# Hybrid decoder layer: expert outputs gated and split into three bf16 parts for a one-hot combination, second-layer bias added once after the expert loop, gates turned ahead of layer two

## The reference, cut to what matters

```python
def expert_block(args):
    xe, e = args
    hid = xe @ w1[e] + b1[e]
    gate = jnp.minimum(hid[:, :D_EXPERT], SWIGLU_LIMIT)
    up = jnp.clip(hid[:, D_EXPERT:], -SWIGLU_LIMIT, SWIGLU_LIMIT)
    act = gate * jax.nn.sigmoid(SWIGLU_ALPHA * gate) * (up + 1.0)
    return act @ w2[e] + b2[e]
yb = lax.map(expert_block, (xb, block_e)).reshape(rows, d) * row_gate[:, None]
return jnp.zeros((n + 1, d), h.dtype).at[row_tok].add(yb)[:n]
```

## Time and profile before

| what | value |
|---|---|
| median of three runs | 1681.19 us (1679.02 to 1683.44) |
| the profiled execution, its own time | 1679.4 us |
| the profiled execution, its span | 1677.6 us |
| PE busy | 1612.6 us (96%) |
| DVE, ACT, POOL busy | 458.6, 316.9, 112.1 us |
| mean granted clock of TensorE | 0.987 |
| chain that ended last | PE 72%, DMA 21%, DVE 4% |
| DMA | 477.32 MB, mean 285 GB/s |

### The profile page before, as it was taken

The page is one execution under the profiler, slowest core; times in us unless marked ns, Lnnn a source line. Parts: engine busy times, 40 slices in busy tenths (PEclk is TensorE's granted clock), DMA queues, the critical chain, the costliest instruction groups (busy, mean ns, idle before and its releaser), DMA issues.

```text
span 1677.6 us, 21022 instructions
## 1 busy us (share of the span) xinstructions
PE 1612.6 (96%) x8487; PEld 751.6 (45%) x8488; DVE 458.6 (27%) x966; ACT 316.9 (19%) x529; POOL 112.1 (7%) x150
## 2 busy tenths in 40 slices
PE   7999999999979999999999999999999999999997
PEld 4677776776555433333333333333333333333332
DVE  3665322224771421111111112111121111112122
ACT  2224131123400131111111111111011111111123
POOL 1322101012150030000000000000000000000000
PEclk9999999999989999999999999999999999999999
DMA  4334212125854579996999999999999979949940
GB/s 160 111 121 128 102 51 102 51 101 163 255 150 168 240 285 420 417 378 258 419 419 416 419 417 418 419 416 419 417 418 419 416 311 364 419 194 408 415 146 31
DMA packets 112366, 477.32 MB, mean 285 GB/s; under 512 B 7386, under 2 KB 18067, under 8 KB 79475
## 3 DMA queue, kind: packets, MB, share of 16 engines
q1 hardware_dynamic: 109846, 467.64, 70.4%
q0 software_dynamic: 2480, 9.11, 1.9%
HBM read 469.72 MB, written 6.62 MB: 284 GB/s over the span
## 4 chain that ended last, share of the span: by engine, by line
PE 72%; DMA 21%; DVE 4%; issue 1%; ACT 1%; SPq 0%; ACTq 0%; DVEq 0%
PE ps L631 69%; DMA arena<-in_moe_w 20%; PE ps L981 1%; ACT arena L1307 1%; PE ps L1053 1%; DVE arena L1525 1%; PE ps L649 0%; DMA arena<-in_state_conv 0%; DVE arena L1620 0%; DVE arena L1559 0%; DVE arena L1522 0%; PE ps L1087 0%; PE ps L703 0%; DVE arena L1563 0%; DVE arena L1589 0%
## 5 line engine op out<-in xcount | busy, mean ns | idle before, releaser
L631 PE MATMUL ps<-arena 128*64 128x512 f32 (+12 forms) x7898 | 1521.4, 476 | 37.8 <-DMA arena<-in_moe_w 17.0
L631 PEld LDWEIGHTS ps<-arena 128*64 128x64 f32 (+6 forms) x7898 | 687.0, 148 | 842.0 <-issue 663.3
L1774 DVE TENSOR_SCALAR arena<-ps 128x512 f32<-128x512 f32 x35 | 24.2, 692 | 446.2 <-PE ps L631 446.2
L1322 ACT ACTIVATE arena<-arena 128x512 f32<-128x512 f32 x35 | 22.0, 630 | 475.4 <-DVE arena L1774 475.4
L1767 DVE COPY arena<-arena 96x64 bf16 x35 | 6.7, 191 | 251.6 <-PE ps L1053 248.1
L1327 ACT ACTIVATE arena<-ps 128x512 f32<-128x512 f32 x35 | 20.9, 597 | 261.6 <-PE ps L631 261.6
L1758 DVE TENSOR_TENSOR arena<-ps,arena 128x512 f32<-128x512 f32 x36 | 24.9, 692 | 122.7 <-PE ps L981 121.6
L1307 ACT ACTIVATE arena<-ps 128x512 f32<-128x512 f32 x36 | 21.5, 597 | 134.4 <-PE ps L631 134.4
L1322 ACT ACT_TABLE_LOAD x35 | 44.9, 1283 | 0.6
L1409 DVE SCALAR_TENSOR_TENSOR arena<-arena 128x344 f32<-128x344 f32 x48 | 35.5, 740 | 1.7
L1120 ACT ACTIVATE arena<-arena 128x1024 f32<-128x1024 f32 (+1 forms) x12 | 12.6, 1052 | 113.8 <-DVE arena L1644 103.3
(11 more groups left out here) (249 smaller groups left out, 649.3 us busy)
## 6 DMA issues: line engine op xcount, KB each, us to landing
arena<-in_moe_w SPq DMA_DIRECT2D x192, 2048.0 KB, 18.3
arena<-in_w_in SPq DMA_DIRECT2D x16, 2048.0 KB, 11.1
arena<-in_state_delta POOLq DMA_DIRECT2D x16, 512.0 KB, 6.3
arena<-in_w_proj_a SPq DMA_DIRECT2D x2, 2048.0 KB, 11.1
out_sd_s<-arena SPq DMA_DIRECT2D x8, 512.0 KB, 5.8
arena<-in_w_proj_b SPq DMA_DIRECT2D x2, 2048.0 KB, 11.5
arena<-in_w_out SPq DMA_DIRECT2D x2, 2048.0 KB, 7.8
arena<-in_ple_gate_w SPq DMA_DIRECT2D x2, 2048.0 KB, 16.0
```

What stands on the lines that cost most here:

```text
L631: return pe.matmul(out, lhsT, rhs, start=first, stop=last, skip_group_check=True)
L1322: ACTF(s_sb, g_sb, ACT.Sigmoid, scale=ALPHA).then_inc(sem("glu_sig_ready"), 1)
L1774: TS(g_sb, ps[:, GATE_B, :], LIMIT, None, ALU.min).then_inc(sem("glu_gate_ready"), 1)
```

## The change

On PE, in a block: `combine` now multiplies a bf16 one-hot `PgT` (1 where a slot takes a token) by three bf16 parts of y that have been multiplied by the slot's gate, so 18 bf16 matmuls in place of 6 f32 ones. The gates are turned directly behind the activation (`turn_gates`), where the rows were turned; the rows are turned between the two units of layer two. The layer-two bias leaves the loop: after it, `gmT` (expert by token, f32, 32 rows) times `b2` is added for all tokens in 6 f32 matmuls ahead of the last `combine`. `b2` is read by one more DMA (128 KB) in front of `ptok`, into the slot of u3, and the PE queue waits for all of `ple_in` before these matmuls, where it waited behind `combine`.

On DVE: a reduce of the turned gates over the tokens gives the slot's gate `gate_col`; `PgT` is "greater than zero" of the same bank; the remainders of the split are made by two more instructions. On ACT: y's copy out of PSUM becomes the scaled first part, and a second part is rounded from the remainder; the copy of `PgT` is gone. `UP_B` is free again for the next block when DVE has made the first remainder (`ysb_ready` at `b * 4 + 2`). At the start, DVE clears four buffers in place of one, and the biases' split on POOL has 2048 columns in place of 3072.

```diff
@@ SP
-            sp.dma_start(b12[0:NE, 2 * D:3 * D], t["moe_b2"][0]).then_inc(sem("router_in"), 16)
@@
             sp.wait_ge(used[uslot[3]], nb)
+            sp.dma_start(b2[0:NE, :], t["moe_b2"][0]).then_inc(sem("ple_in"), 16)
             sp.dma_start(ptok[:, 0:2, :], t["p_prompt"][0, 0].rearrange("(a p) d -> p a d", p=P)).then_inc(sem("ple_in"), 16)
@@ PE
-                pe.wait_ge(sem("ysb_ready"), ready)
-                pe.wait_ge(sem("pgT_ready"), ready)
+                pe.wait_ge(sem("ysb_ready"), ready * 4)
                 for tt in range(2):
+                    for part in y_parts:
+                        for g in range(2):
+                            mm(ps[:, 2 * tt + g, :], PgT[64 * g:64 * g + 64, P * tt:P * tt + P], part[64 * g:64 * g + 64, :], False, True)
+                for part in y_parts:
                     for g in range(2):
-                        mm(ps[:, 2 * tt + g, :], PgT[64 * g:64 * g + 64, P * tt:P * tt + P], y_sb[64 * g:64 * g + 64, :], False, True)
-                for g in range(2):
-                    m = mm(ps[64 * g:64 * g + 64, 4, :], PgT[64 * g:64 * g + 64, 2 * P:TOK], y_sb[64 * g:64 * g + 64, :], False, True)
+                        m = mm(ps[64 * g:64 * g + 64, 4, :], PgT[64 * g:64 * g + 64, 2 * P:TOK], part[64 * g:64 * g + 64, :], False, True)
                 m.then_inc(sem("comb_done"), 1)
+            def turn_gates(b):
+                pe.wait_ge(sem("xsel_ready"), b + 2)
+                pe.wait_ge(sem("pg_ready"), b + 1)
+                for tt, (t0, tn) in enumerate(TILES):
+                    m = pe.transpose(ps[:, TURN_B, t0:t0 + tn], Pg[0:tn, tt, :], ident[0:tn, 0:tn])
+                m.then_inc(sem("pgT_done"), 1)
@@
-                            pe.wait_ge(sem("ysb_ready"), b + 1)
+                            pe.wait_ge(sem("ysb_ready"), b * 4 + 2)
@@
-                turn_rows(b + 2)
+                turn_gates(b)
                 pe.wait_ge(sem("actT_ready"), b + 1)
@@
                     m.then_inc(used[s], 1)
+                    if u == 4:
+                        pe.wait_ge(sem("pgT_ready"), b + 2)
+                        turn_rows(b + 2)
...
-                for g in range(2):
-                    c0 = 2048 + 512 * g
-                    m = mm(ps[64 * g:64 * g + 64, UP_B, :], Ebc[0:96, :], b12s[0:96, c0:c0 + 512], False, True)
-                m.then_inc(sem("y_done"), 1)
-                pe.wait_ge(sem("xselT_ready"), b + 2)
-                pe.wait_ge(sem("pg_ready"), b + 1)
-                for tt, (t0, tn) in enumerate(TILES):
-                    m = pe.transpose(ps[:, TURN_B, t0:t0 + tn], Pg[0:tn, tt, :], ident[0:tn, 0:tn])
-                m.then_inc(sem("pgT_done"), 1)
-
+            pe.wait_ge(sem("ple_in"), 64)
+            for tt in range(2):
+                for g in range(2):
+                    mm(ps[:, 2 * tt + g, :], gmT[0:NE, P * tt:P * tt + P], b2[0:NE, 512 * g:512 * g + 512], False, True)
+            for g in range(2):
+                mm(ps[64 * g:64 * g + 64, 4, :], gmT[0:NE, 2 * P:TOK], b2[0:NE, 512 * g:512 * g + 512], False, True)
             combine(nb + 1)
-            pe.wait_ge(sem("ple_in"), 48)
+            pe.wait_ge(sem("xselT_ready"), nb + 1)
@@ ACT
-                act.wait_ge(sem("y_done"), b + 1)
-                ACTF(y_sb, ps[:, UP_B, :], ACT.Copy).then_inc(sem("ysb_ready"), 1)
-                act.wait_ge(sem("pgT_done"), b + 2)
-                ACTF(PgT, ps[:, TURN_B, 0:TOK], ACT.Copy).then_inc(sem("pgT_ready"), 1)
+                act.wait_ge(used[uslot[5]], b + 1)
+                act.wait_ge(sem("pgT_ready"), b + 2)
+                ACTF(y_parts[0], ps[:, UP_B, :], ACT.Copy, scale=gate_col).then_inc(sem("ysb_ready"), 1)
+                act.wait_ge(sem("ysb_ready"), b * 4 + 6)
+                ACTF(y_parts[1], y_rest, ACT.Copy).then_inc(sem("ysb_ready"), 1)
@@ DVE
-            dve.memset(y_sb, 0.0).then_inc(sem("ysb_ready"), 1)
+            for part in y_parts:
+                dve.memset(part, 0.0).then_inc(sem("ysb_ready"), 1)
+            dve.memset(y_rest, 0.0).then_inc(sem("ysb_ready"), 1)
@@
+                dve.wait_ge(sem("pgT_done"), b + 2)
+                dve.tensor_reduce(gate_col, ps[:, TURN_B, 0:TOK], AX.X, ALU.add).then_inc(sem("gate_col_ready"), 1)
+                TS(PgT, ps[:, TURN_B, 0:TOK], 0.0, None, ALU.is_gt).then_inc(sem("pgT_ready"), 1)
                 rows_turned(b + 2)
+                dve.wait_ge(sem("gate_col_ready"), b + 1)
+                dve.wait_ge(sem("ysb_ready"), b * 4 + 5)
+                STT(y_rest, ps[:, UP_B, :], gate_col, y_parts[0], ALU.mult, ALU.subtract).then_inc(sem("ysb_ready"), 1)
+                dve.wait_ge(sem("ysb_ready"), b * 4 + 7)
+                TT(y_parts[2], y_rest, y_parts[1], ALU.subtract).then_inc(sem("ysb_ready"), 1)
```

More of the change, by code:

```diff
@@ L280, in hybrid_layer @@
         Pg = moe(3, P)
-        PgT = moe(TOK)
+        PgT = moe(TOK // 2).bitcast(BF16)
+        gate_col = moe(1)
         xsel = moe(512)
@@ L286, in hybrid_layer @@
         actT = moe(4, P)
-        y_sb = moe(512)
+        y_parts = [moe(256).bitcast(BF16) for _ in range(3)]
+        y_rest = moe(512)
         fng = view(slot_at[uslot3], D)
         ptok = view(slot_at[uslot3] + D, 3, PLE)
+        b2 = view(slot_at[uslot3] + 2 * D, D)
         pT = moe(2, TOK)
```

14 lines of the change are left out of this document (7 added, 7 removed).

## The result

The changed kernel takes **1673.59 us** (median; 1670.38 to 1678.32), the kernel before 1681.19. The ratio to the kernel before, measured beside it, is 0.9954 with a 95% interval of 0.9937 to 0.9972. The forecast was 1680.3 us and its range began at 1674.5: the change is faster by some 7 us, where 0.9 was forecast.

A forecast was written before the change was run, and what follows sets the result against it. PE was taken to bound the loop's outer stretches, the weight stream its middle. Blocks .58 us shorter gave 2.5 us at the end, less 1.6 for the clock: .9 off 1681.19, so 1680.3 us, range 1674.5 to 1688.

The forecast's parts named there:

- The bias's smaller split on POOL and one DMA less lie far from the path: 0.: At the start, before the loop: POOL's narrower split and the dropped DMA were to change the time by 0.
- The two regimes: Expert loop: PE sets the pace at 28.45 us per block, or the weight stream does at 30.12 us per expert.
- The stall of `UP_B`: In each block, PE's first layer-one step on that bank was to wait .10 us, from 0 to .30.
- d: Saving per block of the expert loop: .48 combination plus .20 turns less .10 stall, .58 us, making a block 27.87.
- rival 3: Loop and tail: no stall, bf16 steps at .213, clock stays up; .86 us saved per block, 1674.9 us; chance .11.
- The first stretch: Blocks 0 to 5 and block 6 up to u4's release: PE sets the pace unless blocks save above 1.0 us.
- Start: Before the router: DVE's extra clears cost .6 us against .32 of slack, so the router waits .3 longer.
- End: Behind the loop: stream restarts 7.0 us earlier, PE idles 2.9 before the bias, gain 2.5 before the clock's charge.
- The clock: Tail, bias and last combination: PE's stop drops the granted clock to half, charged at 1.6 us.
- Rival 1: Combination in each block: weight loads set the bf16 step at .37 us, a slower kernel at 1696; chance .13.
- rival 2: In each block, the handover of `UP_B` costs .6 us rather than .1, giving 1684.7 us; chance .10.
- Rival 4: Middle of the loop: the stream's 30.12 us follow PE's pace, so 20 blocks gain 12 us more, 1668; chance .02.

The follow-up runs named there:

- e1: The changed kernel with POOL's split of the biases back at 3072 columns and the DMA of b2 that feeds it: 1684.78 us, ratio 1.0029.
- e4: The kernel before with one added wait, putting POOL's bias split behind the sums of the position mixing: 1670.67 us, ratio 0.9946.
- e5: The changed kernel with its combination in f32 again (one f32 sum, f32 one-hot matrix): 1680.65 us, ratio 1.0007.
- first group: The first group of runs of the unmodified change against the kernel before: 1673.59 us, ratio 0.9954.
- second group: A second group of runs of the same changed kernel, as control, against the kernel before: 1673.53 us, ratio 0.9962.
- e2: The changed kernel with b2 read early by POOL's queue and the wait for ple_in back behind the last combination: 1666.31 us, ratio 0.9922.
- e11: The changed kernel with b2 read early, the bias split deferred, and bias matmuls over 128 rows (gates times .25): 1663.53 us, ratio 0.9897.
- e6: The changed kernel with only two of the three bf16 parts of y combined: 1666.07 us, ratio 0.9927.
- e3: The changed kernel with five extra unused f32 matmuls on PE ahead of the wait for ple_in: 1673.28 us, ratio 0.9957.
- e7: The changed kernel with b2 read early and POOL's bias split behind the position mixing's sums: 1662.54 us, ratio 0.9894.
- e10: The changed kernel with b2 read early, the split deferred, and the four long bias matmuls in four groups of 32 rows: 1662.88 us, ratio 0.9900.

## Why the prediction was wrong

**"The bias's smaller split on POOL and one DMA less lie far from the path: 0."** This step failed, and it alone is nearly the measured difference: 6.3 us between the mixing and the loop. POOL itself is far from the path, as the earlier trace rows and its idle time suggested; but its instructions hold up DVE's additions of two SBUF tiles, .69 us without and 2.5 to 6.3 us with it, and there DVE is what PE waits for: one wait of 9.1 us before and of 2.3 or 3.8 after. e1 puts the wide split back and loses the gain; e4 takes the split out of the way in the kernel before and has it without the change. The Trainium skill (SBUF — State Buffer, "Who interferes with whom") says just this: a DVE instruction with two SBUF inputs contends with a GpSimd instruction that reads SBUF, and it calls the contention an exclusive lock. The trace agrees: the additions last until POOL's instruction has ended, and those from PSUM keep .68 us. An instruction's cost was looked for on its own engine only.

**Block.** The two regimes were right, and so was the stream's 30.12 us; PE's distance is 27.57 and not 27.87. Of the terms, the combination was mis-sized: 2.19 us, not 2.45, a saving of .74 and not .48 (e5 has the old 2.93 back at 1304.47 to 1307.40). The steps run at the lower end of the range given, .21, and entering and leaving costs less than .35. Turns: the gates take .65 (1307.09 to 1307.74) and the rows .69 with the entry, 1.34 against 1.35. The stall of `UP_B`: e5 has no remainder to wait for and its blocks are .67 and not .74 longer, so .07 against .10. d is .87, the .86 of rival 3.

**The first stretch.** PE was expected to set the pace there up to d = 1.0, and d is .87. But in the first group's profile block 5 waits 1.3 us for the stream (the DMA at 715.78 in the chain; its distance is 28.89 us, the others' 27.57), so the restart gained 1.3 less than 6 d. The lead of 5 us was mis-sized: u3 was put at 741 and landed at 740.8, but with a loop that started 2.3 us earlier (587.00 against 589.31). In the kernel before that is about 743, a lead of 3.1 us, an estimate, and five blocks use it up at d = .6 already. In the second group's profile the block doesn't wait, so the changed kernel stands at the border.

**Start.** +.3 as said. From the first clear to the copy of the logits it is 569.22 - 567.77 = 1.45 us, where it was 573.15 - 572.01 = 1.14:

```profile
567.77 0.82 DVE L1693 MEMSET arena<- 128x256 uint32 x3
...
569.22 0.42 DVE L1699 COPY arena<-ps 32x320 f32<-32x320 f32 x1
```

**End.** The landing of `ple_in`, counted from the loop's start, moved by 7.4 us (1021.8 to 1014.4) against 7.0, two errors that cancel: the restart came earlier than said, since d is larger, and the way from `ple_w` to the last landing took longer. The queue of SP, answering:

```profile
1580.67 5.41 SPq L497 DMA_DIRECT2D arena<-in_ple_w  x1
1586.12 1.23 SPq L500 DMA_DIRECT2D arena<-in_moe_b  x1
...
1589.44 0.58 SPq L503 DMA_DIRECT2D arena<-in_final_norm_g  x1
```

From `ple_w` to the last issue it is 8.77 us against 7.40 before (1592.52 to 1599.92), and the last read takes 12.0 against 11.2: 2.2 together, where .3 were charged. Not all of it is `b2`'s: the four kernels that read `b2` elsewhere and early have 8.8 + 11.0 us (e2) and 7.9 + 11.7 (e11), 19.5 to 19.8 in all, against 20.8 in the changed kernel and 18.6 before. So about 1 us is `b2`'s, and what the rest is stays open. PE's last layer-two step, at 1020.2 us from the loop's start before, now stands at 1596.40 - 587.00 = 1009.4, 10.8 earlier where 8.0 and the .3 of the start were said. So PE stands idle for 5.1 to 5.7 us, not 2.9.

**The clock.** 1.6 us were charged, as what a stop of 2.8 us had cost at 431.6. Bias and combination take 13.1 us and 6.8 with the clock up (e11), so it was 6.3. The stop does come with a fall, as said: in both profiles the clock is down before the first bias matmul. What failed is the size: at 435.8 the clock stood at half for some 3 us, and here it does for 13.6, through the whole stage. And the stop is only a part of the cause: with none in front of it the clock falls in the bias as well (e2, where the stage takes 9.8 us, 3.0 more than in e11), and over 128 rows it doesn't (e11). Whether the 32 rows also kept the clock down behind the stop is not shown: no run has a stop with 128-row matmuls behind it. The rule of the Trainium skill that the prediction cited (TensorE: Matmul & The Clock Gate, "HAM oscillation — how this bites in real kernels"), of a wait for a DMA that halves the rate, agrees with the changed kernel's profiles and not with e2, where PE was busy throughout. The rows at 431.6 don't bear it out as cleanly as the prediction said: that stop was a wait for DVE, and the clock was still at 1.00 when PE went on at 434.48, with f32 matmuls of 32 rows, and fell 1.1 us later.

**Together.** Expected were +.3 from the mixing to the loop, and -1.2 from there to the transposes. Measured were -6.3 and +1.9 to +2.8: the idle time is 2.2 to 2.8 more and the clock 4.7 more than said, against 2.5 that PE is earlier (3.9 in the second group) and .4 by which bias and combination are cheaper. In the profiled pair of the first group the rest hid this: there the two executions differ by 1.1 us, since the part ahead of the mixing was 3.9 us longer in the later one. Not closed: the medians of e1 and the changed kernel differ by 11 us, the middle columns of their profiles by 6.3 and 7.4.

**Rivals.** Rival 1 (the loads set the step) is refuted by the combination's 2.19 us, rival 2 (the handover) by the stall of .07. Rival 3 had the block right and the clock wrong; its 1674.9 is near the measured time by luck, since its gain was to come from the blocks and the tail, and loop and tail together lost. Rival 4 (the 30.12 us follow PE) is refuted, also by e5 and e6. None had the front in it. By e1 the change proper would have been slower by .3%, as the upper tail of the forecast. The three parts do gain their 7 us (e5), but the tail takes them back, and what is left is about what the narrower split gives.

## What to carry to other kernels

Before an edit off the critical path is costed at nothing, look at what runs beside it on the other engines, not only at who waits for it: the durations of one and the same instruction (here .69 to 6.28 us on one line) show at once where an engine holds up another. A wait that is moved in front of other work is costed with everything that is queued ahead of the last transfer it counts, and work that leaves a loop for its tail stands there without cover; reading its operand early (e2, 5 to 7 us) is worth more than filling the gap (e3, nothing in the medians). e7 has both the early read and the deferred split, and no kernel here is faster: 1662.5 us, 1.06% less than before.

## What the hardware showed that was not expected

- POOL's bias split, on 32 rows, stretched DVE's 128x512 f32 additions of two SBUF tiles from .69 to as much as 6.38 us (e1), and left those with a PSUM operand at .68.
- The granted clock fell to half during f32 matmuls of 32 rows that followed each other without a gap (e2 and e7, one execution each), and stayed at full through the same matmuls on 128 rows (e11), and where four groups of 32 rows worked at once and were through in 1.08 us (e10).
- In a stop of 5.1 us the clock fell, and it stayed at half for 13.6 us, the whole of bias and combination. In the kernel before it fell 1.1 us behind a stop of 2.9 us and stayed at half for some 3 us.
- Four f32 matmuls of 32 rows and 128 columns in four row groups took 1.08 us from the first load to the next stage's; one behind the other .91 each.
- The combination's three bf16 parts cost 2.19 us against 2.93 in f32, three quarters of the time for three times the matmuls.
